# Scan heads of a hybrid decoder step: sample value rows ahead of the chunk states, the copy of the sample outputs later

## The reference

```python
proj = h @ w_in                                  # q, f, i (values), z (gate)
q = silu(q); f = lb + (1 - lb) * sigmoid(f + b_f); k = 1 - f; v = i
o, S = hgrn2_scan(q, k, v, log(f), s0)           # S_t = diag(f_t) S_{t-1} + k_t v_t^T,  o_t = S_t^T q_t
y = (rmsnorm(o, g_norm_w) * silu(z)) @ w_out
```

## Time and profile before

| | |
|---|---|
| median of 3 runs | 1120.97 us (1120.49 to 1121.94) |
| the profiled execution | 1122.75 us, span of its records 1121.1 us |
| mean granted TensorE clock | 0.995 of full |
| TensorE matmul busy | 1089.2 us, 97% |
| TensorE weight load busy | 1038.6 us, 93% |
| VectorE, ScalarE, GpSimd busy | 635.8, 505.1, 151.0 us |
| HBM traffic | 124.00 MB read, 22.02 MB written, 130 GB/s over the span |

### The profile page before, as it was taken

One profiled execution on the slowest core, in us unless ns is written; L12 is line 12 of the kernel. 1 busy time (PEld: TensorE's weight loads), 2 busy tenths in 40 slices (PEclk: granted clock), 3 DMA queues, 4 the chain that ended last, 5 costly groups with the idle time before them and its releaser, 6 DMA issues.

```text
span 1121.1 us, 26202 instructions
## 1 busy us (share of the span) xinstructions
PE 1089.2 (97%) x11121; PEld 1038.6 (93%) x11121; DVE 635.8 (57%) x1280; ACT 505.1 (45%) x1035; POOL 151.0 (13%) x156
## 2 busy tenths in 40 slices
PE   8999999999999999998999999999999999999998
PEld 6799999999999998988998999999999999998997
DVE  3776676767585858673446634652455246437332
ACT  4653444445453545541124643653464365447122
POOL 1000010100000000000000730351045006300000
PEclk9999999999999999998999999999999999999999
DMA  9763444444544442219324455325623652263441
GB/s 321 282 206 110 142 134 149 137 144 128 153 126 147 134 136 77 81 52 273 104 76 142 117 134 152 100 71 118 166 77 97 152 138 80 60 156 87 152 113 47
DMA packets 232219, 147.73 MB, mean 132 GB/s; under 512 B 7876, under 2 KB 226206, under 8 KB 231591
## 3 DMA queue, kind: packets, MB, share of 16 engines
q1 hardware_dynamic: 217456, 134.17, 42.4%
q10 hardware_dynamic: 14646, 11.89, 3.2%
HBM read 124.00 MB, written 22.02 MB: 130 GB/s over the span
## 4 chain that ended last, share of the span: by engine, by line
PE 85%; DVE 6%; ACT 3%; issue 2%; DMA 2%; SPq 1%; ACTq 0%; DVEq 0%
PE PJ L382 26%; PE PJ L1707 18%; PE PJ L1415 15%; PE PJ L403 7%; PE X L1273 2%; PE X L1835 1%; PE X L1393 1%; PE X L1214 1%; PE X L1862 1%; PE PJ L685 1%; PE X L1395 1%; DMA pre<-in_ada_w_dram 1%; SPq L2521 1%; PE PJ L429 1%; PE X L1800 1%
## 5 line engine op out<-in xcount | busy, mean ns | idle before, releaser
L355 DVE TENSOR_TENSOR w_lo<-raw,w_hi 128x1024 fp32r<-128x1024 f32 (+1 forms) x128 | 157.0, 1239 | 163.0 <-ACT w_hi L347 162.1
L347 ACT ACTIVATE w_hi<-raw 128x1024 fp32r<-128x1024 f32 (+1 forms) x128 | 129.3, 1025 | 167.7 <-PE PJ L1707 69.9
L1707 PE MATMUL PJ<-w_hi,h_hi 128*128 128x256 f32 x600 | 167.3, 287 | 2.1 <-issue 1.4
L1707 PE MATMUL PJ<-w_lo,h_hi 128*128 128x256 f32 x600 | 164.6, 283 | 0.0
L382 PE MATMUL PJ<-h_hi,w_hi 128*128 128x288 f32 (+1 forms) x736 | 160.7, 300 | 0.6 <-ACT v_ L939 0.6
L382 PE MATMUL PJ<-h_hi,w_lo 128*128 128x288 f32 (+1 forms) x736 | 157.7, 296 | 0.0
L382 PE MATMUL PJ<-h_lo,w_hi 128*128 128x288 f32 (+1 forms) x736 | 157.4, 295 | 0.0
L1707 PE MATMUL PJ<-w_hi,h_lo 128*128 128x256 f32 x480 | 135.8, 283 | 0.0
L382 PEld LDWEIGHTS PJ<-h_hi,w_hi 128*128 128x128 f32 x736 | 118.1, 189 | 4.6 <-issue 3.1
L382 PEld LDWEIGHTS PJ<-h_hi,w_lo 128*128 128x128 f32 x736 | 118.9, 189 | 0.0
L382 PEld LDWEIGHTS PJ<-h_lo,w_hi 128*128 128x128 f32 x736 | 118.8, 189 | 0.0
(11 more groups left out here) (346 smaller groups left out, 2149.2 us busy)
## 6 DMA issues: line engine op xcount, KB each, us to landing
raw<-in_a_w_in_dram SPq DMA_DIRECT2D x48, 512.0 KB, 5.0
raw<-in_b_w_in_dram SPq DMA_DIRECT2D x64, 256.0 KB, 3.7
raw<-in_ada_w_dram SPq DMA_DIRECT2D x28, 512.0 KB, 3.9
kvc<-in_cache_kv_w_dram SPq DMA_DIRECT2D x24, 512.0 KB, 5.9
pre<-in_ada_w_dram SPq DMA_DIRECT2D x16, 512.0 KB, 10.1
s<-in_state_hgrn_dram SPq DMA_DIRECT2D x8, 1024.0 KB, 8.2
out_hgrn_sample_dram<-s ACTq DMA_DIRECT2D x8, 1024.0 KB, 5.0
raw<-in_a_w_out_dram SPq DMA_DIRECT2D x16, 512.0 KB, 5.0
```

The source lines that it names most:

```text
L347: act.activation(w_hi[:, i % SPLITS, 0:size], raw[:, n % RAWS, 0:size], ACT.Copy).then_inc(hi_done, 1)
L355: dve.tensor_tensor(w_lo[:, i % SPLITS, 0:size], raw[:, n % RAWS, 0:size], w_hi[:, i % SPLITS, 0:size].bitcast(F32), ALU.subtract).then_in ...
L1707: last = pe.matmul(PJ[:, tile // 2, tile % 2 * 256:tile % 2 * 256 + 256], a, b[:, k, :], start=(first and k == 0 and i == 0), stop=(kk == ...
```

## The change

TensorE's list in steps 1 to 7: the samples' value rows (ticket 3) now stand between the sample output rows and the chunk states. Before they stood behind `pe_seq_out`. ACT's list in the same steps: the copy to `os_` stood ahead of the last three exponentials; it now stands behind them and behind the low half of the samples' values. No instruction is added or taken away, and the semaphores are the same.

```diff
+            def sample_out():
+                act.wait_ge(os_ready, g + 1)
+                if g >= 1:
+                    act.wait_ge(fin_done, 2 * g)
+                act.activation(os_[:], X[:, 2, 384:512].rearrange("p (j t) -> p j t", j=2), ACT.Copy).then_inc(os_done, 1)
...
                 act.wait_ge(orow_ready, g + 1)
                 act.activation(orow[:], X[:, 2, 0:ADV], ACT.Copy).then_inc(orow_done, 1)
-                act.wait_ge(os_ready, g + 1)
-                if g >= 1:
-                    act.wait_ge(fin_done, 2 * g)
-                act.activation(os_[:], X[:, 2, 384:512].rearrange("p (j t) -> p j t", j=2), ACT.Copy).then_inc(os_done, 1)
+                if not new:
+                    sample_out()
             if new:
                 level_exps(5 if scan else 6, XS)
             if new:
...
                 low_half(h, PJ[:, 2, 0:ADV], v_low[:])
+                if scan:
+                    sample_out()
                 if h < AH - 1:
                     act.wait_ge(raw_used, 4 + 4 * h)
                     act.activation(adr[:], PJ[:, 3, :], ACT.Copy).then_inc(adr_done, 1)
...
             if scan and new:
                 pe_seq_rows(pe, g)
+            if new:
+                project_rows(ticket_w(h, 3), keys, [CH], lambda c: PJ[:, 2, 0:ADV])
+            if scan and new:
                 pe_chunk_states(pe, g)
                 pe_seq_out(pe, g)
             if new:
-                project_rows(ticket_w(h, 3), keys, [CH], lambda c: PJ[:, 2, 0:ADV])
                 project_T(ticket_w(h, 4), ("w", h, 4))
```

## The result

| | before | changed |
|---|---|---|
| median | 1120.73 us (4 runs, 1120.45 to 1121.94) | 1114.71 us (4 runs, 1113.72 to 1115.41) |
| profiled execution, span | 1122.75, 1121.1 us | 1114.26, 1112.6 us |

The ratio is 0.9944, with a 95% interval of 0.9928 to 0.996: faster by 6.0 us, 0.56%. The forecast was 1114.7, with a range of 1112.0 to 1117.0. That it fits so well is partly luck: two terms of the sum were off in opposite ways, as the experiments show.

A forecast was written before the change was run, and what follows sets the result against it. TensorE, busy for 97% of the span, was taken to bound the kernel. Gains of 2.6 us in steps 1 to 6 and 3.65 in step 7 make 6.3, so 1120.97 - 6.3 = 1114.7 us, range 1112.0 to 1117.0.

The forecast's parts named there:

- 2.6 us in steps 1 to 6: Gain from TensorE's filled stalls in steps 1 to 6: 2.9 + 0.5 - 6 x 0.13 = 2.6 us.
- The 0.20 behind the sample rows: In each of steps 1 to 6, what follows the sample rows pays 0.20 us even with no wait.
- The 1.89 for the chunk states behind other work: Chunk states behind other matmuls were priced at 1.89 us, not 1.96, from a row of step 8.
- 3.65 us in step 7: Gain in step 7: 2.0 us from filling the stall and 1.66 us from the clock.
- The 1.66 of the clock: Step 7 at full clock: 1.30 us won on L1273 and 0.36 on L1282.
- 1 us on each side for the second fall: Allowance for a varying clock fall after a stall at the start of the output projection: 1 us each way.
- ACT's moved copy costs nothing: ACT's later copy to `os_` ends 6 us before TensorE's next need of it, L1290, so it costs nothing.
- The chunk states' results come later without harm: Chunk states end 1.5 us later; DVE waits 0.2 and ends the recurrence with 4.9 us to spare before L1290.
- The larger stall: Rival: steps 1 to 6 win the weight loads' whole gap, 6.0 us, in all 9.65, time 1111.3; chance 0.09.
- The clock falls all the same: Rival: the clock still falls in step 7, gain 4.6 us, time 1116.4; chance 0.09.
- given back: Rival: another engine sets the step and TensorE waits as long elsewhere, time 1121; chance 0.08.
- slower: Rival: ACT's moved wait delays the splits, TensorE waits before L1290, 3.5 us more, time 1124.5; chance 0.04.

The follow-up runs named there:

- the keys first: The kernel before with ACT's copy of the keys put ahead of its copy of the values: 1115.85 us, ratio 0.995.
- step 7 alone: The changed kernel with TensorE's new order kept only in step 7, ACT's list as changed in all steps: 1119.24 us, ratio 0.998.
- steps 1 to 6 alone: The changed kernel with TensorE's order of before in step 7, ACT's list as changed: 1118.03 us, ratio 0.9966.
- the split ahead: The changed kernel with DVE's split of weight piece (out0, 1, 1) ahead of its wait for x from DRAM: 1111.85 us, ratio 0.9914.
- The order alone: The kernel before with only TensorE's list changed, ACT's list as before: 1117.79 us, ratio 0.9968.
- ACT's list alone: The changed kernel with TensorE's order of before, so only ACT's list is changed: 1122.49 us, ratio 1.0008.

## Why the prediction was right, and where it was off

*TensorE stands still for the keys, and the order hides it.* Right: the stall is gone in all seven steps, and moving the keys' copy alone removes it in six and halves it in the seventh.

*2.6 us in steps 1 to 6.* The mechanism is right and the size too low: 3.7 us in the trace, 3.8 measured alone. The step at fault is the price of the passages. The 0.20 behind the sample rows is close (2.11 for L403, against 1.96 + 0.20), and with the keys first the chunk states behind the sample rows take 1.92, which is 1.73 + 0.19. The 1.89 for the chunk states behind other work is not: it measured 1.73. The row that I took it from was held up by the keys. In the same stretch of the kernel before, ACT's copy of the keys ends at 482.19:

```profile
481.59 0.60 ACT L943 ACTIVATE kr<-X 128x512 f32<-128x512 f32 x1 [0.59 <-PE X L1240]
```

and the first of its chunk states starts at 482.29 in the timeline, so they stood behind their own keys. The list of waits of TensorE has no entry for it, and I did not read the rows of the other engine. Step 7 of the changed kernel bears this out. There the chunk states stand behind L403 as in step 3, but the keys end at 441.85, just ahead of them, and they take 1.97 instead of 1.73:

```profile
441.26 0.59 ACT L949 ACTIVATE kr<-X 128x512 f32<-128x512 f32 x1
```

So the passage was not new. The 1.96 us of the earlier trace rows already held 0.23 us over the 1.73, and with the keys first 0.19 of it is there with no wait. The change moves this price from the chunk states to L403 and does not add one, as the prediction's sum had it. That is why a step wins a little more than its stall, not a little less.

*3.65 us in step 7.* The 2.0 of the stall is right (1.9). The 1.66 of the clock is right for the execution that was profiled and wrong for the median. The prediction took it off 1120.97, although the profiled execution lay 1.8 us above that. The runs near that median were not profiled, but their times are those of the executions without the fall, so they had probably none to give back. An estimate for the mean: with the fall in about 12 of 27 executions it is worth 0.44 x 1.7 = 0.75 us, and 3.7 + 1.9 + 0.75 makes 6.4 us, beside the 6.0 and 6.6 that were measured. The Trainium skill (TensorE: Matmul & The Clock Gate, Part 1) says that the number of slow matmuls at the start of one and the same kernel varies between runs. The traces here show such a variation in the middle of a kernel: the same stall of 2.1 us, with 3.26, 2.68 and twice 1.97 us for the same eight matmuls. I gave it only to the width of the range and not to this term. The two errors, 1.1 us too little in steps 1 to 6 and up to 1.7 too much in step 7, all but cancelled; that the time was met to the tenth is luck.

*1 us on each side for the second fall.* Too narrow. Added up over windows of 1 us, the fall at the output projection costs 3.4 us in ten of the thirteen profiles, 1.7 in those of step 7 alone and steps 1 to 6 alone, and nothing with the split ahead.

*ACT's moved copy costs nothing.* Right: no wait at L1296, and the copy ends at 227.84 with ticket 4 just begun. But the cover that I named, L1290, was not the nearest. The order alone shows that the split for ticket 5 is. It had a slack of 1.7 us in the kernel before. Counted from the end of the sample rows, the new order alone makes the split 1.3 us later and the need 0.6 us earlier, which uses the slack up. Without ACT's part the gain is 3.6 us, and the forecast of 6.3 would have missed by about 3 us.

*The chunk states' results come later without harm.* Right: DVE takes them at 227.17, has the recurrence done at 229.14, and L1296 wants it at 233.96.

*The rivals.* The larger stall, 9.65 us, did not come. Against the weight loads' gap of 1.0 us a step the gain was 0.62, nearer to the matmuls' 0.57. The rule on weight loads (the Trainium skill, Perfetto Trace Analysis, Identifying the Most-Contended Engine) is one on how busy the engine is; read as a measure of a gap it would have misled here. "The clock falls all the same", "given back" and "slower" did not come either.

## What to carry to other kernels

Independent work of the same engine, put into a repeated stall, gives back about the stall that the matmuls show (here 0.62 us for 0.57), not the wider gap of the weight loads. Where the stall is a wait for one operand, try first whether its copy can go ahead on the other engine: here that won 5.6 us with two copies exchanged. A cover that the engine used to have must be followed to its nearest need, which is found by asking what the late engine has queued next, not only what waits for the moved instruction. Before a passage between two kinds of work is priced from a row elsewhere, look at whether the operands of that row were ready. And a gain that hangs on the clock belongs only to those executions in which the clock fell: take it from a profiled execution that has the fall, and from the median only by the share of executions that have it.

## What was unexpected of the hardware

A fall of TensorE's clock behind a short stall came in some executions of one kernel and not in others: at the same stall of 2.1 us in two of four profiles of the kernel before, and at the end of the attention in those of three edited kernels but in none of the kernel before. Where it came in step 7, L1273 and L1282 took up to 1.66 us longer. In one edited kernel with the same stall, ACT's list alone, it came too, and in another, steps 1 to 6 alone, it did not. What decides it was not settled: since the unchanged kernel shows both, no single profile of an edited kernel tells whether its edit made the difference. No profile has a fall behind the stalls of 0.5 to 0.6 us of steps 1 to 6.
